# The last 256 tokens' feed-forward by token rows, in three rounded products with 512 weight columns moving

## The reference

```
n2 = _rmsnorm(h, norm2_w)
ffn = (silu(n2 @ w_gate) * (n2 @ w_up)) @ w_down      # 1024 -> 2816 -> 1024
return (h + ffn)[:, 16:]
```

## Time and profile before

| | |
|---|---|
| median of 3 runs | 2492.4 us (2489.91 to 2498.71) |
| profiled execution | 2494.28 us |
| its span, first to last instruction | 2492.5 us |
| mean granted TensorE clock | 0.914 |
| PE, DVE, ACT busy | 2098.9, 1340.6, 931.1 us |

### The profile page before, as it was taken

One profiled execution on the slowest core, in us unless ns is written; L12 is line 12 of the kernel. 1 busy time (PEld: TensorE's weight loads), 2 busy tenths in 40 slices (PEclk: granted clock), 3 DMA queues, 4 the chain that ended last, 5 costly groups with the idle time before them and its releaser, 6 DMA issues.

```text
span 2492.5 us, 30084 instructions
## 1 busy us (share of the span) xinstructions
PE 2098.9 (84%) x10828; PEld 1283.2 (51%) x10828; DVE 1340.6 (54%) x3170; ACT 931.1 (37%) x2322; POOL 599.0 (24%) x570
## 2 busy tenths in 40 slices
PE   5999999998786756556556898899999986999999
PEld 3877557776442311111112443356666553678888
DVE  7743764454776677877777767765344333121000
ACT  3124445523444333333334567834444112431000
POOL 0000000000444454435444334333333220000000
PEclk9999999999888887877778899899999998999999
DMA  8821002232999999999999999999999993324544
GB/s 332 304 68 68 1 26 68 60 101 67 394 420 420 420 416 415 421 421 415 414 399 420 393 351 414 380 419 419 418 418 418 418 418 122 112 67 141 154 153 152
DMA packets 124448, 712.65 MB, mean 286 GB/s; under 512 B 14688, under 2 KB 16864, under 8 KB 58512
## 3 DMA queue, kind: packets, MB, share of 16 engines
q0 software_dynamic: 74608, 542.25, 52.9%
q1 hardware_dynamic: 49456, 168.38, 19.6%
q10 hardware_dynamic: 240, 0.16, 0.0%
HBM read 708.61 MB, written 2.13 MB: 285 GB/s over the span
## 4 chain that ended last, share of the span: by engine, by line
PE 57%; DMA 25%; DVE 7%; ACT 6%; issue 3%; POOL 2%; ACTq 0%; SPq 0%; DVEq 0%
DMA arena<-experts,eidx 24%; PE psum L1150 11%; PE psum L892 9%; PE psum L633 6%; PE psum L634 6%; PE psum L635 5%; DVE arena L1746 4%; PE psum L1163 3%; POOL arena L1716 2%; PE psum L1132 2%; PE psum L1009 2%; PE psum L959 2%; ACT sq L1417 1%; PE psum L745 1%; PE psum L721 1%
## 5 line engine op out<-in xcount | busy, mean ns | idle before, releaser
L892 PE MATMUL psum<-arena,sq 64*64 64x512 f32 x4096 | 630.1, 741 | 318.4 <-ACT sq L1417 308.5
L1746 DVE CUSTOM_DVE_ANT_0 arena<-arena 128x1024 f32<-128x1024 f32 x560 | 679.0, 1223 | 359.1 <-DMA arena<-experts,eidx 328.7
L1716 POOL DMA_INDIRECT arena<-experts,eidx x512 | 582.9, 1138 | 949.3 <-PE psum L892 764.5
L892 PEld LDWEIGHTS psum<-arena,sq 64*64 64x64 f32 x4096 | 153.3, 155 | 704.0 <-ACT sq L1417 470.3
L1403 ACT ACTIVATE arena<-arena 128x2 f32<-128x2 f32 x256 | 52.0, 203 | 709.3 <-DVE arena L1746 707.5
L1150 PE MATMUL psum<-n_t,ring 128*128 128x256 f32 x1408 | 313.9, 382 | 2.3 <-DVE n_t L1743 2.3
L1150 PEld LDWEIGHTS psum<-n_t,ring 128*128 128x128 f32 x1408 | 264.3, 190 | 65.9 <-issue 30.5
L633 PE MATMUL psum<-hn_high,w_high 128*128 128x512 f32 (+1 forms) x432 | 179.6, 416 | 13.7 <-DVE hn_low L1743 12.4
L634 PE MATMUL psum<-hn_low,w_high 128*128 128x512 f32 (+1 forms) x432 | 174.5, 404 | 0.0
L635 PE MATMUL psum<-hn_high,ring_low 128*128 128x512 f32 (+1 forms) x432 | 172.8, 400 | 0.0
L1417 ACT ACTIVATE sq<-sq,arena 128x64 f32<-128x64 f32 x512 | 150.3, 340 | 24.4 <-ACT arena L1409 0.7
(11 more groups left out here) (289 smaller groups left out, 2723.9 us busy)
## 6 DMA issues: line engine op xcount, KB each, us to landing
ring<-w_stream SPq DMA_DIRECT2D x264, 512.0 KB, 4.2
arena<-w_ada SPq DMA_DIRECT2D x48, 512.0 KB, 6.2
arena<-experts,eidx POOLq DMA_INDIRECT x512, 12.4
arena<-cum_rows POOLq DMA_DIRECT2D x1, 2112.0 KB, 9.6
x<-xT SPq DMA_DIRECT2D x1, 2048.0 KB, 14.9
arena<-rel_rows POOLq DMA_DIRECT2D x1, 2048.0 KB, 12.6
outT<-hn_rest SPq DMA_DIRECT2D x16, 128.0 KB, 5.9
arena<-sub_keys POOLq DMA_DIRECT2D x1, 1024.0 KB, 6.2
```

Of the source, the lines that this page charges most:

```text
L892: last = mm(bank(4 + 2 * odd + a)[HALF * b:HALF * b + HALF, :], diag[k, s, :], rows[k, s, D + a * 512:D + (a + 1) * 512], start=c == 0, st ...
L1716: nc.gpsimd.indirect_dma_start(rows[:, s, :], None, experts, bass.IndirectOffsetOnAxis(ap=eidx[:, n // P % 2, n % P:n % P + 1], axis=0)).t ...
L1746: return V.tensor_tensor_reduce(out=out, in0=a, in1=b, scale=1.0, scalar=0.0 if op1 == ALU.add else -TAKEN, op0=op0, op1=op1, accum_out=accum)
```

## The change

In `block2(1)` the feed-forward after the norm is replaced on all engines; the first half of the tokens is left as it is. The token rows now stand and the weights move: for a token tile of 128 and a group of 512 inner columns (the last group has 256) the gate products fill one bank per token tile and the up products another. Weights are stored once more in DRAM in an order for this (66 tiles of 512 KB: per group and matrix 4 tiles of 2 slices by 512 columns, or 2 tiles of 4 slices by 256; then 22 tiles for the two halves of the down projection), and the old order of these weights is still streamed for the first half. Each tile is rounded by ACT into `last_high` (4 slots in the arena) and split by DVE, two tiles ahead. The normed activations are split into `n_high` and `n_low`, the products of silu and up come out by token rows (`act_rows`), are turned by PE with f32 transposes during the next group, and rounded and split into `act_high` and `act_low`. x is turned as well, into `x_rows`, for the last addition. The output of this half is stored by token rows, 4 stores of 256 KB into a tensor of its own; the host puts the two halves together.

```diff
+GROUPS = [(512 * g, min(512, FF * P - 512 * g)) for g in range(-(-FF * P // 512))]
+LAST = FIRST_BLOCK + BLOCK + B_UP
...
-        claim(("norm2",), 3 if g == 0 else 4)
+        claim(("norm2",), 3 if g == 0 else 0)
+        if g:
+            claim(("x rows",), 4, 5, 6, 7)
+            claim(("last",), 0, 1, 2, 3)
...
+def last_tiles():
+    order = []
+    for j, (_, width) in enumerate(GROUPS):
+        per = D // width
+        for up in range(2):
+            order += [("gate up".split()[up], j, at, per) for at in range(KT // per)]
+    return order + [("down", c, at, 2) for c in range(2) for at in range(FF // 2)]
...
+TURNS = {(last_tile("gate", j + 1, 1) if j + 1 < len(GROUPS) else last_tile("down", 0, 1)): j for j in range(len(GROUPS))}
...
 # SyncE: the stores
+            for c in range(2):
+                for t in range(2):
+                    store_rows(c, t)
...
 # TensorE, in block2, for g == 1 after the mean squares
+                def last_rows():
+                    taken("x rows")
+                    for t in range(2):
+                        for k in range(KT):
+                            last = nc.tensor.transpose(bank(4 + 2 * t + k // 4, P, k % 4 * P),
+                                                       x[:, k, lo + t * P:lo + (t + 1) * P], ident[:])
+                        last.then_inc(x_turned.sem, 1)
+                    taken("last")
+                    for i, (name, j, at, per) in enumerate(LAST_TILES):
+                        n = LAST + i
+                        pe.wait_ge(w_split.sem, w_split.ready(FIRST_BLOCK + i))
...
+                        for c in range(per):
+                            k = at * per + c
+                            if name == "gate" and j == 0:
+                                pe.wait_ge(n_split.sem, n_split.ready(k))
+                            if name == "down" and j == 0 and k % 4 == 0:
+                                pe.wait_ge(act_split.sem, act_split.ready(2 * (k // 4) + 1))
+                            for t in range(2):
...
+                                last = product(out, part(rows_of, ALL, k, tokens), part(w, ALL, c), k == 0, k == ks - 1)
+                        last.then_inc(tile_done.sem, 1)
+                        if i in TURNS:
+                            j = TURNS[i]
+                            for t in range(2):
+                                pe.wait_ge(act_done.sem, act_done.ready(2 * j + t))
...
+                                for f in range(GROUPS[j][1] // P):
+                                    last = nc.tensor.transpose(bank(4 + t, P, f * P), act_rows[:, t, f * P:(f + 1) * P],
+                                                               ident[:])
+                                last.then_inc(act_turned.sem, 1)
...
 # ScalarE
+                def last_highs(i):
+                    n = LAST + i
+                    if i < len(LAST_TILES):
+                        act.wait_ge(ring_ready[n % SLOTS], 16 * (n // SLOTS + 1))
+                        act.wait_ge(tile_done.sem, tile_done.ready(n - SLOTS))
+                        op(last_high[:, n % SLOTS, :], ring[:, n % SLOTS, :], ACT.Copy).then_inc(w_rounded.sem, 1)
+                def last_rows():
+                    for k in range(KT):
+                        act.wait_ge(nt_ready.sem, nt_ready.ready(3 * KT + k))
+                        op(n_high[:, k, :], n_t[:, k, 0:PAIR], ACT.Copy).then_inc(n_rounded.sem, 1)
+                    for i in range(len(LAST_TILES)):
+                        if i in (1, 2):
+                            act.wait_ge(x_turned.sem, x_turned.ready(i - 1))
+                            op(x_rows[:, i - 1, :], psum[:, (2 + 2 * i) * 512:(4 + 2 * i) * 512], ACT.Copy)\
+                                .then_inc(x_taken.sem, 1)
+                        for j, (_, width) in enumerate(GROUPS):
+                            if i == last_tile("gate", j) + 1:
+                                act.wait_ge(tile_done.sem, tile_done.ready(LAST + i - 1))
+                                for t in range(2):
...
+                                    op(silu_rows[:, t, 0:width], bank(t, width), ACT.Silu).then_inc(silu_done.sem, 1)
+                        if i - 1 in TURNS:
...
+                                act.wait_ge(act_turned.sem, act_turned.ready(2 * j + t))
+                                op(act_high[:, fs, t * P:(t + 1) * P],
+                                   bank(4 + t, GROUPS[j][1]).rearrange("p (f m) -> p f m", m=P), ACT.Copy)\
+                                    .then_inc(act_rounded.sem, 1)
+                        last_highs(i + 2)
...
+                if g:
+                    last_highs(0)
+                    last_highs(1)
                 root(0, PAIR, "norm2")
...
 # VectorE
+                def last_rows():
+                    last_lows(0)
+                    last_lows(1)
+                    roots(10)
+                    for k in range(KT + 2):
+                        if k < KT:
+                            scaled(k, n_t[:, k, 0:PAIR], x[:, k, tokens], N2).then_inc(nt_ready.sem, 1)
+                        if k >= 2:
+                            dve.wait_ge(n_rounded.sem, n_rounded.ready(k - 2))
+                            V.tensor_tensor(n_low[:, k - 2, :], n_t[:, k - 2, 0:PAIR], n_high[:, k - 2, :].bitcast(f32),
+                                            ALU.subtract).then_inc(n_split.sem, 1)
+                    for i in range(len(LAST_TILES) + 1):
+                        for j, (_, width) in enumerate(GROUPS):
+                            if i == last_tile("up", j) + 1:
+                                dve.wait_ge(tile_done.sem, tile_done.ready(LAST + i - 1))
...
+                        if i - 1 in TURNS:
...
+                        for c in range(2):
+                            if i == last_tile("down", c) + 1:
...
+                                for t in range(2):
+                                    V.tensor_tensor(out_rows[:, 2 * c + t, :], bank(6 + t if c == 0 else t),
+                                                    x_rows[:, t, c * 512:(c + 1) * 512], ALU.add).then_inc(o_ready.sem, 1)
+                        last_lows(i + 2)
```

More of the change, by code:

```diff
@@ L154, in bank_claims @@
             claim(("out", m), (1, 2)[m % 2] if g == 0 else m % 4)
-        claim(("norm2",), 3 if g == 0 else 4)
[L156 to L161, removed]
+        claim(("norm2",), 3 if g == 0 else 0)
+        if g:
+            claim(("x rows",), 4, 5, 6, 7)
+            claim(("last",), 0, 1, 2, 3)
+        else:
+            for t in range(2 * FF):
+                claim(("up", t), 1 + t % 3)
+            for m in range(KT):
+                claim(("down", m), 1 + (2 * FF + m) % 3)
             ours = count[0]
@@ L408, in program @@
                   + [inside(tail_of_hn, f * PAIR, PAIR) for f in range(6)])
+        last_high = over("last_high", [P, SLOTS, D], "arena", start=0)
+        assert rows_at % 8 == 0 and h_tok_at % 8 == 0
+        act_high = over("act_high", [P, FF, PAIR], "arena", start=rows_at)
+        act_low = over("act_low", [P, FF, PAIR], "arena", start=rows_at + FF * PAIR)
+        n_high = over("n_high", [P, KT, PAIR], "arena", start=rows_at + 2 * FF * PAIR)
+        n_low = over("n_low", [P, KT, PAIR], "arena", start=rows_at + (2 * FF + KT) * PAIR)
+        act_rows = inside(arena, rows_at + 2 * (FF + KT) * PAIR, 2, 512)
+        assert 2 * (FF + KT) * PAIR + 1024 <= SLOT * 2 * D
+        silu_rows = inside(tail_of_hn, 0, 2, 512)
+        x_rows = inside(arena, h_tok_at, 2, D)
+        out_rows = inside(arena, h_tok_at + 2 * D, 4, 512)
         psum = ctx.enter_context(nc.psum_tensor("psum", [P, 8 * 512], f32))
@@ L603, in _ @@
                 if late >= 0 and late % 3 == 0 and late < 3 * KT:
-                    store(0, late // 3)
+                    store(late // 3)
                 eng.wait_ge(tile_done.sem, tile_done.ready(n - SLOTS))
@@ L607, in _ @@
                     t = LAST_ORDER[t]
+                if g == 1 and t >= B_UP:
+                    t += BLOCK - B_UP
                 eng.dma_start(ring[:, n % SLOTS, :], w_stream[n if n < FIRST_BLOCK else FIRST_BLOCK + t])\
                    .then_inc(ring_ready[n % SLOTS], 16)
-            for m in range(KT):
-                store(1, m)
+            for c in range(2):
+                for t in range(2):
+                    store_rows(c, t)
             for a in range(2):
-                eng.wait_ge(out_stored[a], 16 * KT)
+                eng.wait_ge(out_stored[a], 16 * (KT // 2 + 2))
         @block.tensor
@@ L2047, in scaled, with last_lows @@
                     return stt(out, of, vec[:, gain_at + k:gain_at + k + 1], root2[0][:, 0:of.shape[-1]], ALU.mult, ALU.mult)
+                def last_lows(i):
+                    n = LAST + i
+                    if i < len(LAST_TILES):
+                        dve.wait_ge(w_rounded.sem, w_rounded.ready(FIRST_BLOCK + i))
+                        V.tensor_tensor(ring_low[:, n % SLOTS, :], ring[:, n % SLOTS, :],
```

(17 more changed lines are left out.)

80 lines of the change are left out of this document (73 added, 7 removed).

## The result

The changed kernel takes 2455.22 us in the median of 4 runs (2452.25 to 2461.37) against 2493.11 for the kernel before; the ratio is 0.9846, 95% interval 0.9825 to 0.9866. That is 37.9 us less; the prediction was 2458, a gain of 34.4. Its profiled execution took 2461.37 us, the slowest of the four; so a comparison of the two profiled executions alone would give 32.9 us.

What follows compares the result with a forecast made beforehand. PE alone bounds the last stage: 228.2 us out, 191.0 in (183.8 products, 6.1 turning, 1.1 waiting), start +1.2, end +1.3, difference -34.7 us, so 2458 us from the median 2492.4; range 2446 to 2474.

Steps and rivals of the forecast that it cites:

- The bound and the pace: Last stage: only PE's work counts; products at 0.2317 us (512 columns) and 0.119 (256) take 183.8 us, not 228.2.
- Rival 1: Last-stage products: streamed columns set the pace at 0.216 us, 11.7 us more gain, 2446 us; chance 6%.
- rival 4: Last-stage matmuls: standing-operand loads of 0.19 us lie in the open, 160 us for 840, 2617 us; chance 3%.
- Turning: Before the down projection: 44 PE transposes of activations, 4.8 us, plus 1.3 us at six cuts; 6.1 us in sum.
- the third tile: Start of the last stage: PE waits 1.1 us for the split of tile 2, wanted at 2268.1 and ready at 2269.1.
- The switch of kind: At the turns: first product after a small f32 matmul takes 0.34 us instead of 0.23, twice at each of six cuts.
- The splitting beside it: Last-stage weight tiles: ACT rounding and DVE splitting take a 6.1 us way, hidden under 8.3 us of PE; costs nothing.
- rival 2: At the last stage's turns: hand-overs not hidden, about 1 us wait each, later splits, clock dips; 2466 to 2480 us; 15%.
- Rival 3: Last-stage ring loop sets the pace, PE waits at every tile and its clock falls; 2533 or 2567 us; chance 3%.
- The start: Before the first last-stage product: rounding, splits, three scalings and one subtraction delay PE to 2262.55 us, +1.2 us.
- The end: After the last product: two additions of 0.69 us and a 256 KB store of 2.9 us; 4.3 us, +1.3.
- rows 5: Profile rows before the change: 48 matmuls with 256 weight columns moving and token columns standing take 5.71 us, 0.119 each.

Runs made afterwards that it cites:

- the run with three slots: Changed kernel with each last-stage weight tile loaded one tile later, so two PE tiles and not three cover its way; tail 210.36 us, median 2468.98 us.
- two products: Changed kernel with the third product (activation remainder by rounded weights) left out throughout the last stage; tail 157.96 us, median 2423.15 us.
- the two runs: Rounding without the layout, on the kernel before: 2456.48 us, ratio 0.9861; token-row layout without rounding, on the changed kernel: 2498.68 us, ratio 1.0025.

## Why the prediction was right

**The bound and the pace.** PE alone decides the stage, before and after. The products follow as forecast; PE's timeline with 42 products of 512 columns between the first two rows, 24 of 256 between the next two, and a turn of 4 transposes (start, length):

```profile
2275.73 0.40 PE L688 MATMUL psum<-last_high,n_high 128*128 128x512 f32 x1
...
2285.47 0.40 PE L688 MATMUL psum<-last_high,n_high 128*128 128x512 f32 x1
...
2390.64 0.28 PE L688 MATMUL psum<-last_high,n_high 128*128 128x256 f32 x1
...
2393.47 0.28 PE L688 MATMUL psum<-last_high,n_high 128*128 128x256 f32 x1
...
2399.38 0.60 PE L1041 MATMUL psum<-ident,arena 128*128 128x128 f32 x4
2399.74 0.47 PE L688 MATMUL psum<-last_high,act_high 128*128 128x512 f32 x1
2400.05 0.39 PE L689 MATMUL psum<-ring_low,act_high 128*128 128x512 f32 x1
```

(2285.47 - 2275.73) / 42 = 0.2319 us, forecast 0.2317; (2393.47 - 2390.64) / 24 = 0.118, forecast 0.119. 744 * 0.2319 + 96 * 0.118 = 183.9 us of the 189.4.

**Rival 1** (0.216 us) and **rival 4** (weight loads in the open) are excluded by these rows.
The Trainium skill's sustained 131 ns for 512 columns (TensorE: Matmul & The Clock Gate, section Back-to-back issue gap) is not what any product here shows either; its N / 2.4 + 2.5 for the isolated gap is 7% short of 0.2319.

**Turning.** Forecast 6.1 us, measured 4.7 by the run without them and 5.2 as what the products and the third tile leave of the 189.4. The switch of kind costs less than I took: 2399.38 to 2399.74 for four transposes, and 0.31 us to the next product instead of 0.23, once per cut and not twice.

**The splitting beside it.** Hidden, as followed through. The way was put at 6.1 us and is 6.3 by the run with three slots, 5.9 in the median when counted off; **rival 2** needed 1 us at each turn, and the run without turns and the run that rounds twice show none. **Rival 3** needs a way above 8.4 us at tile after tile; the longest single one in the changed kernel's trace is 7.7. ACT and DVE were busy for 83.5 and 97.7 us in the stage, where I had near 90 and near 107, and the DMA share was 0.57 and not 0.62.
The Trainium skill's warning of a clock that falls tile after tile (same page, section HAM oscillation) did not come true, even where PE really waited at tiles: with three slots and with two products the granted clock of the stage was 1.00, with single waits of PE of at most 1.3 and 2.0 us.

**The start.** The timeline at the start; between the last two rows lies PE's wait for the third tile:

```profile
2263.27 1.91 PE L1000 MATMUL psum<-ident,x 128*128 128x128 f32 x16
2263.47 0.47 ACT L1586 ACTIVATE rstd<-psum,eps 128x256 f32<-128x256 f32 x1 [0.53 <-PE psum L991]
...
2264.51 1.28 DVE L1894 SCALAR_TENSOR_TENSOR n_t<-x,vec,rstd 128x256 f32<-128x256 f32 x3
...
2266.04 0.48 DVE L1894 SCALAR_TENSOR_TENSOR n_t<-x,vec,rstd 128x256 f32<-128x256 f32 x1
...
2266.27 0.47 PE L688 MATMUL psum<-last_high,n_high 128*128 128x512 f32 x1 [1.09 <-DVE n_low L2218]
...
2266.77 0.48 DVE L1894 SCALAR_TENSOR_TENSOR n_t<-x,vec,rstd 128x256 f32<-128x256 f32 x1
...
2270.88 1.23 DVE L2205 TENSOR_TENSOR ring_low<-ring,last_high 128x1024 fp32r<-128x1024 f32 x1 [0.42 <-ACT last_high L1550]
...
2271.69 0.39 PE L690 MATMUL psum<-last_high,n_low 128*128 128x512 f32 x1
...
2272.16 0.50 PE L688 MATMUL psum<-last_high,n_high 128*128 128x512 f32 x1
```

From the square root to the first product 2.80 us, before 1.69: +1.1, forecast +1.2. The wait ahead of the third tile is 2272.16 - 2271.69 - 0.23 = 0.24 us, and 0.1 more at the product behind it, where I had 1.1: DVE delivers a slice every 2266.77 - 2266.04 = 0.73 us and not every 0.84, as its operations overlap at their ends and I had added their full lengths.

**The end.** Timeline of the last matmul, the two additions and the two stores:

```profile
2455.26 0.40 PE L690 MATMUL psum<-last_high,act_low 128*128 128x512 f32 x1
2455.69 1.29 DVE L2245 TENSOR_TENSOR arena<-psum,arena 128x512 f32<-128x512 f32 x2 [4.70 <-PE psum L690]
2456.41 0.93 SPq L633 DMA_DIRECT2D last_out<-arena  x2
```

From the end of the last product (2455.67) to the end of the span 3.93 us, before 3.0: +0.9, forecast +1.3. The last store takes 2459.6 - 2456.98 = 2.6 us with 256 KB, as 2.55 with 128 KB; I had 2.9.

**The sum.** By the tail: forecast -34.7, measured -36.7. The 2 us are 0.9 from the turns, 0.8 from the third tile and 0.4 from the end (and 0.1 each way from the pace and the start). What the median adds (37.9) is within the spread of the part ahead.

**What the forecast didn't ask.** It priced the change as a whole and never the rounding by itself. With its own rows 5 it could have: 1584 * 0.119 = 188.5 us for weights standing, if the pace holds with the operands exchanged (it does, 0.118), next to 183.8 + 6.1 = 189.9 for token rows. The gain was known; which edit it belongs to was only shown by the two runs.

## What to carry to other kernels

Where an f32 matmul is bound by PE, price the products before the layout: three rounded ones (3 * 0.118 = 0.354 us with 256 columns) in place of one f32 matmul (0.432) brought all of the gain here, and exchanging the standing and the moving operand brought none of it. Work for ACT and DVE that is new beside a PE-bound stage costs nothing while the way of a tile (landing, rounding, splitting) fits in the tiles of PE that are buffered; work that way out as a sum, since it is also what decides once PE gets faster. And where the part ahead of an edit moves from run to run by more than the differences that are asked about, compare from a fixed event in the profile to the end: two profiles of one kernel agreed to 0.1 us in that, while its single runs lay between 2451.8 and 2461.4.

## What was not expected of the hardware

- A rounded product costs 0.2319 us with 512 columns and 0.118 with 256. The difference over 256 columns makes 0.445 ns a column, 1.07 cycles at 2.4 GHz, and only some 4 ns are fixed; an f32 record of 256 columns takes 0.216 us, 2.02 cycles a column, so an f32 matmul, two records, 4.05. Three rounded products are 3.3 cycles a column, and that ratio is nearly the whole gain. A narrower matmul loses hardly anything, and the 7% over a column a cycle grow with the columns. What takes them was not tried. The width of the standing part it is not: the profile of before has a tile with 8 standing columns, here the first and the last of 22 products in a row (start, length),

```profile
158.86 0.40 PE L633 MATMUL psum<-hn_high,w_high 128*8 128x512 f32 x1
...
163.73 0.39 PE L633 MATMUL psum<-hn_high,w_high 128*8 128x512 f32 x1
```

and (163.73 - 158.86) / 21 is 0.2319 us again.
- The landing of a 512 KB tile rose from 3.5 to 4.4 us in the median when the stage moved 222 GB/s (two products) instead of 175 (changed kernel), well under the 420 GB/s that the page shows in the gather stage.
- The same idle time of PE (2.84 and 2.83 us) was followed by a granted clock of 0.50 in one kernel, after 2.1 us of products with idle time between them, and of 1.00 in another, with products on end. One profile of each doesn't show whether that is the reason.
